# A gate matmul as seven products over halves of 256 tokens, with its weight parts made in gaps of GpSimd

## The reference, cut to what matters

```python
# x: (4096 tokens, 1024), float32; one layer
n = rmsnorm(h)
z = n @ w_in                                  # q, k, v, gates, and 4 x 512 columns of the convolution
y_gla  = rmsnorm(chunked_linear_attention(q, k, v, log_a)) * silu(g_gla)
y_conv = cb * causal_conv3(cc * cu) * silu(g_conv)
h = h + concat([y_gla, y_conv]) @ w_out
gate = sigmoid(h @ w_ple_gate + b_ple_gate)   # 1024 x 1024: what the change is about
h = h + gate * (p @ w_ple)                    # p has 256 columns
out = rmsnorm(h) * final_norm_w
```

## Time and profile before

| | us |
|---|---|
| median of three runs | 2034.15 (2034.09 to 2035.0) |
| the profiled execution, its own time | 2032.89 |
| its span | 2031.1 |
| TensorE busy | 1997.4 (98%) |
| VectorE / ScalarE / GpSimd busy | 1231.7 / 726.2 / 577.5 |

### The profile page before, as it was taken

One profiled execution on the slowest core, in us unless ns is written; L12 is line 12 of the kernel. 1 busy time (PEld: TensorE's weight loads), 2 busy tenths in 40 slices (PEclk: granted clock), 3 DMA queues, 4 the chain that ended last, 5 costly groups with the idle time before them and its releaser, 6 DMA issues.

```text
span 2031.1 us, 25878 instructions
## 1 busy us (share of the span) xinstructions
PE 1997.4 (98%) x9732; PEld 1665.8 (82%) x9732; DVE 1231.7 (61%) x1512; ACT 726.2 (36%) x1123; POOL 577.5 (28%) x590
## 2 busy tenths in 40 slices
PE   6999999999999999999999999999999999999997
PEld 5888888888888888888888888888888888888886
DVE  5766667666653576576576576567565355555553
ACT  5354354444433432332332332322322233333332
POOL 3766666666651112112112112144511000000000
PEclk9999999999999999999999999999999999999999
DMA  6345354454446312127312127486677322222111
GB/s 228 136 162 202 140 187 175 148 198 160 165 186 260 145 62 88 58 104 284 109 63 88 57 104 285 172 302 243 236 254 287 107 94 94 93 93 89 62 73 45
DMA packets 83991, 306.73 MB, mean 151 GB/s; under 512 B 10128, under 2 KB 20800, under 8 KB 73408
## 3 DMA queue, kind: packets, MB, share of 16 engines
q1 hardware_dynamic: 54752, 179.17, 24.2%
q0 software_dynamic: 29152, 126.40, 17.2%
HBM read 183.90 MB, written 121.63 MB: 150 GB/s over the span
## 4 chain that ended last, share of the span: by engine, by line
PE 96%; DVE 2%; ACT 1%; issue 1%; SPq 0%; DMA 0%; DVEq 0%; ACTq 0%
PE bank L1079 15%; PE bank L1085 15%; PE bank L1081 15%; PE bank L825 14%; PE bank L833 14%; PE bank L826 14%; PE bank L1166 1%; PE bank L1164 1%; PE bank L1165 1%; PE bank L912 1%; PE bank L972 1%; PE bank L963 1%; PE bank L856 1%; DVE XL L1581 1%; PE bank L857 1%
## 5 line engine op out<-in xcount | busy, mean ns | idle before, releaser
L1079 PE MATMUL bank<-XH,WC 128*128 128x512 f32 x1344 | 524.3, 390 | 0.1
L1085 PE MATMUL bank<-XL,WC 128*128 128x512 f32 x1344 | 523.0, 389 | 0.2 <-DVE XL L1747 0.2
L1081 PE MATMUL bank<-XH,WC 128*128 128x512 f32 x1344 | 522.9, 389 | 0.0
L1747 DVE TENSOR_TENSOR XL<-RQ,XH 128x1024 fp32r<-128x1024 f32 x168 | 220.0, 1344 | 230.4 <-ACT XH L1423 229.3
L1085 PEld LDWEIGHTS bank<-XL,WC 128*128 128x128 f32 x1344 | 252.3, 188 | 53.0 <-DVE XL L1747 0.6
L1079 PEld LDWEIGHTS bank<-XH,WC 128*128 128x128 f32 x1344 | 252.4, 188 | 52.3 <-issue 0.5
L1081 PEld LDWEIGHTS bank<-XH,WC 128*128 128x128 f32 x1344 | 252.4, 188 | 51.4
L763 POOL TENSOR_TENSOR RQ<-RQ 128x1024 f32<-128x1024 f32 x48 | 116.7, 2454 | 416.4 <-DVE RQ L1766 405.2
L1423 ACT ACTIVATE XH<-RQ 128x1024 fp32r<-128x1024 f32 x168 | 170.7, 1053 | 166.9 <-PE bank L1085 148.7
L825 PE MATMUL bank<-XH,WG 128*128 128x512 f32 x512 | 199.2, 389 | 0.0
L826 PE MATMUL bank<-XH,WG 128*128 128x512 f32 x512 | 199.2, 389 | 0.0
(11 more groups left out here) (185 smaller groups left out, 3330.0 us busy)
## 6 DMA issues: line engine op xcount, KB each, us to landing
WC<-w_scratch SPq DMA_DIRECT2D x21, 2048.0 KB, 8.8
RQ<-n_scratch POOLq DMA_DIRECT2D x32, 1024.0 KB, 5.5
w_scratch<-prep_hi POOLq DMA_DIRECT2D x84, 256.0 KB, 2.3
w_scratch<-PB POOLq DMA_DIRECT2D x84, 256.0 KB, 2.3
n_scratch<-raw SPq DMA_DIRECT2D x8, 2048.0 KB, 7.1
y_scratch<-y_sb SPq DMA_DIRECT2D x64, 256.0 KB, 2.8
RQ<-y_scratch POOLq DMA_DIRECT2D x16, 1024.0 KB, 6.3
xt<-xb_dram SPq DMA_DIRECT2D x64, 256.0 KB, 5.1
```

The costliest lines, as they stand in the source:

```text
L1079: nc.tensor.matmul(bank[:], WC[:, i, q, 0, k], xh, start=(k == 0 and i in (P1, P2, P5)), stop=False, skip_group_check=True)
L1081: nc.tensor.matmul(bank[:], WC[:, i, q, 1, k], xh, start=False, stop=False, skip_group_check=True)
L1085: mm = nc.tensor.matmul(bank[:], WC[:, i, q, 0, k], xl, start=False, stop=(k == 3), skip_group_check=True)
L1747: nc.vector.tensor_tensor(XL[:, k], RQ[:, OPERAND[s % 7], 2 * h:2 * h + 2], XH[:, k].bitcast(F32), ALU.subtract).then_inc(sx_lo, 1)
```

## The change

- The gate is computed per block of 512 tokens by the same seven products, over two halves of 256 tokens (`HT`) and two halves of the features. A matmul has 256 columns. `XHg` and `XLg` hold two operands each, over the old `XH` and `XL`. The tables T1 to T4 are made by VectorE in `TA` and `TB_`.
- The per-layer product is made in 8 units of 12 matmuls of 256 columns, two behind each of P2, P5, P3 and P4. A unit is two output tiles of one half of the tokens.
- Sums, sigmoids, mixing and squares go by unit. The loops over pairs of blocks are gone: all 8 blocks are written out.
- The gate's weights are now a fourth set of seven parts in `w_scratch`. The parts of P1, P2 and P4 are plain quarters; GpSimd makes them as 24 strips of 128x256, three in each convolution step (`strip`), in buffers over those of the heads' output. Those of P7, P6, P3 and P5 are made in steps 8 to 10 (`late_load`, `late_part`, 20 entries in the slots). The two tiles of `w_ple` follow in step 11 (`prep_tile`).
- In step 11 SyncE loads seven chunks of 2 MB and two of 1 MB.
- The statistics of the last block are one matmul after the last addition; before, seven of the eight squares went in earlier.

Core of the diff:

```diff
+HT = TB // 2
+GATE_A = (3, 4)
+GATE_C = (0, 1)
+PLE_BANK = (6, 7, 2)
+RESULT = ((0, 0), (1, 1), (1, 0), (0, 1))
...
-TILES = {GLA: 14, GATE: 16}
+TILES = {GLA: 14}
 PREP_STORES = (1, 1, 2, 2, 1, 7)
-GATE_TILES = PLE_K + KT
-GATE_SLOTS = {NB: (0, 0, 1), NB + 1: (1, 2, 1), NB + 2: (2, 2, 1)}
+PLAIN = ((P1, 0, 0), (P2, 0, 1), (P4, 1, 1))
+STRIPS = 4 * 2 * len(PLAIN)
+GATE_SLOTS = {NB: (1, 1, 1), NB + 1: (5, 3, 1), NB + 2: (5, 2, 1)}
+LATE_STORES = (0, 0, 2, 1, 1, 4)
 C_W0, C_W1, C_W2, C_GATED = range(1, 5)
...
@@ -459,14 +529,11 @@
                 if g % NP < NP - 1:
                     return
                 sp.wait_ge(sx_free, 4 * (7 * g + i + 1))
-                if g < STEPS - 1:
-                    if i == P1:
-                        wait_prepared(sp, g // NP + 2)
-                    load_weights(g // NP + 1, i)
-                elif i < 5:
-                    tile = WP[:] if i == 0 else WG[:, 2 * i - 2:2 * i]
-                    sp.dma_start(tile.bitcast(F32), g_scratch[i].rearrange("p (m h k c) -> p m h k c", m=2, h=2, k=KT)
-                                 ).then_inc(w_chunk[i], 16)
+                if i == P1:
+                    wait_prepared(sp, g // NP + 2)
+                    if g == STEPS - 1:
+                        sp.wait_ge(tile_stored, 16 * 2 * STRIPS)
+                load_weights(g // NP + 1, i)
...
-                    for half in range(2):
-                        sp.wait_ge(tile_lo_stored[half], 16 * GATE_TILES // 2)
+                    sp.wait_ge(tile_stored, 16 * 2 * (STRIPS + PLE_K))
...
+                if g == STEPS - 1:
+                    next_weights(g, P4)
+                    for part, tile in enumerate((WPH, WPL)):
+                        sp.dma_start(tile[:].bitcast(F32), g_scratch[part].rearrange("p (k m c) -> p k m c", k=PLE_K, m=KT)
+                                     ).then_inc(wp_loaded, 16)
...
                 for n in range(sum(counts), sum(counts) + GATE_SLOTS[g][slot_of]):
-                    prep_tile(n)
+                    if n % 5 == 0:
+                        late_load(n // 5)
+                    else:
+                        late_part(n // 5, n % 5 - 1)
...
+            def piece(n, src, raw_buf, hi_buf, hi_dst, lo_dst):
+                if n > 0:
+                    pool.wait_ge(tile_stored, 16 * 2 * n)
+                pool.dma_start(raw_buf, src).then_inc(tile_loaded, 16)
+                pool.wait_ge(tile_loaded, 16 * (n + 1))
+                pool.tensor_scalar(hi_buf, raw_buf, 1.0, 0.0, ALU.mult, ALU.add).then_inc(tile_split, 1)
+                pool.wait_ge(tile_split, 2 * n + 1)
+                pool.dma_start(hi_dst, hi_buf.bitcast(F32)).then_inc(tile_stored, 16)
+                pool.tensor_tensor(raw_buf, raw_buf, hi_buf.bitcast(F32), ALU.subtract).then_inc(tile_split, 1)
+                pool.wait_ge(tile_split, 2 * n + 2)
+                pool.dma_start(lo_dst, raw_buf).then_inc(tile_stored, 16)
+            def strip(n):
+                q, (i, tile, half), c = n // 6, PLAIN[n // 2 % 3], n % 2
+                if n == 0:
+                    for h in range(2):
+                        pool.wait_ge(y_stored[h], y_count(0))
+                at_col = half * TB + c * HT
+                to = 2 * q * TB + c * HT
+                piece(n, pair_tiles(3, q)[tile][:, at_col:at_col + HT], strip_raw[:], strip_hi[:],
+                      w_scratch[3, i, :, to:to + HT], w_scratch[3, i, :, to + TB:to + TB + HT])
+            def prep_tile(m):
+                if m == 0:
+                    wait_prepared(pool, 4)
...
                 difference(g, Q12, Q12, t3_made)
-                if g in GATE_SLOTS:
-                    prep_tiles(g, 0)
+                if is_conv(g):
+                    for n in range(3 * g, 3 * g + 3):
+                        strip(n)
+                elif g in GATE_SLOTS:
+                    gate_parts(g, 0)
+                elif g == STEPS - 1:
+                    for n in range(PLE_K):
+                        prep_tile(n)
                 split_waits(s + P6)
-                if g in GATE_SLOTS:
-                    prep_tiles(g, 1)
                 pool.wait_ge(t4_made, 2 * (g + 1))
                 difference(g, Q11, Q11, t1_made)
                 if g == STEPS - 1:
@@ -795,10 +934,12 @@
                 split_waits(s + P5)
                 load_quadrant(g + 1, Q11)
                 if g in GATE_SLOTS:
-                    prep_tiles(g, 2)
+                    gate_parts(g, 1)
                 split_waits(s + P3)
                 pool.wait_ge(t1_made, 2 * (g + 1))
                 load_quadrant(g + 1, Q22)
+                if g in GATE_SLOTS:
+                    gate_parts(g, 2)
                 split_waits(s + P4)
                 load_quadrant(g + 1, Q21)
...
+            def gate_product(b, i):
+                z = 7 * b + i
+                banks = GATE_A if i in (P1, P6, P7, P4) else GATE_C
+                for q in range(4):
+                    if b == 0 and q == 0:
+                        pe.wait_ge(w_chunk[i], 16 * 4)
+                    if q % 2 == 0:
+                        wait_gate_bank(b, i, q // 2)
+                    if q == 0:
+                        pe.wait_ge(gx_hi, z + 1)
+                    acc_ap = ps[banks[q // 2]][:, q % 2 * HT:q % 2 * HT + HT]
+                    for k in range(4):
+                        xh, xl = XHg[:, z % 2, k], XLg[:, z % 2, k]
+                        nc.tensor.matmul(acc_ap, WC[:, i, q, 0, k], xh, start=(k == 0 and q % 2 == 0 and i in (P1, P2, P5)),
+                                         stop=False, skip_group_check=True)
+                        nc.tensor.matmul(acc_ap, WC[:, i, q, 1, k], xh, start=False, stop=False,
+                                         skip_group_check=True)
+                        if q == 0 and k == 0:
+                            pe.wait_ge(gx_lo, z + 1)
+                        mm = nc.tensor.matmul(acc_ap, WC[:, i, q, 0, k], xl, start=False, stop=(k == 3),
+                                              skip_group_check=True)
+                    mm.then_inc(g_prod, 1)
...
+            def gate(b):
+                gate_product(b, P1)
+                gate_product(b, P6)
+                if b > 0:
+                    out_stats(b - 1)
+                gate_product(b, P7)
+                for c, i in enumerate((P2, P5, P3, P4)):
+                    gate_product(b, i)
+                    ple_unit(b, 2 * c)
+                    ple_unit(b, 2 * c + 1)
...
+            def gate(b):
+                z = 7 * b
+                gate_hi(z + P6)
+                gate_copy(b, P1, 0)
+                gate_copy(b, P1, 1)
+                gate_hi(z + P7)
+                gate_copy(b, P6, 0)
+                gate_copy(b, P6, 1)
+                gate_hi(z + P2)
+                split_p_hi(b)
+                if b > 0:
+                    nc.scalar.preload_act_table_set(LOG_EXP)
+                    out_rms(b - 1)
+                gate_hi(z + P5)
+                sigmoid(b, 0)
+                gate_copy(b, P7, 0)
+                sigmoid(b, 1)
+                gate_copy(b, P7, 1)
+                gate_hi(z + P3)
+                gate_square(b, 0)
+                gate_square(b, 1)
+                sigmoid(b, 2)
+                sigmoid(b, 3)
+                gate_hi(z + P4)
+                gate_square(b, 2)
+                gate_square(b, 3)
+                sigmoid(b, 4)
+                sigmoid(b, 5)
+                gate_hi(z + 7)
+                sigmoid(b, 6)
+                gate_square(b, 4)
+                sigmoid(b, 7)
+                if b == NB - 1:
+                    nc.scalar.preload_act_table_set(LOG_EXP)
+                gate_square(b, 5)
+                gate_square(b, 6)
+                gate_square(b, 7)
             def out_rms(b):
...
+            def gate(b):
+                z = 7 * b
+                gate_lo(z + P6)
+                gate_lo(z + P7)
+                gate_t1_t4(b)
+                gate_lo(z + P2)
+                split_p_lo(b)
+                if b > 0:
+                    dve.wait_ge(out_rstd, b)
+                    final_norm(b - 1, range(4))
+                gate_lo(z + P5)
+                if b > 0:
+                    final_norm(b - 1, range(4, 8))
+                gate_sum(b, 0)
+                gate_sum(b, 1)
+                gate_lo(z + P3)
+                gate_mix(b, 0)
+                gate_mix(b, 1)
+                gate_sum(b, 2)
+                gate_sum(b, 3)
+                add_square(b, 1)
+                gate_lo(z + P4)
+                gate_mix(b, 2)
+                gate_mix(b, 3)
+                gate_t3(b + 1)
+                gate_sum(b, 4)
+                gate_sum(b, 5)
+                add_square(b, 3)
+                gate_lo(z + 7)
+                gate_mix(b, 4)
+                gate_mix(b, 5)
+                gate_t2(b + 1)
+                add_square(b, 4)
+                add_square(b, 5)
+                gate_mix(b, 6)
+                gate_mix(b, 7)
```

(81 more changed lines are left out.)

556 lines of the change are left out of this document (322 added, 234 removed).

## The result

| | before | after |
|---|---|---|
| median of six runs each, us | 2034.12 (2032.46 to 2036.19) | 2049.28 (2044.16 to 2050.46) |
| ratio to before | | 1.0071 (95% interval 1.0058 to 1.0084) |
| span of the profiled execution | 2031.1 | 2048.4 |

What follows compares the result with a forecast made beforehand. The prediction took TensorE's own stream, 96% of the chain, as the bound. Its terms -20.5 + 17.8 + 2.0 + 4.8 + 3.6 gave +7.7 us, 2042 us against 2034.15, 0.4% slower, range 2034 to 2059.

Steps and rivals of the forecast that it cites:

- its own case: Whole kernel: the forecast's terms as summed, 2042 us, with 2036 to 2049 for this case alone; chance kept 0.55.
- a gate whose pace VectorE sets: Gate: a wait in front of one VectorE sum holds all behind it, +17 us, 2059; chance 0.10.
- the rival at 2049: Convolution: strips' instructions beside VectorE's additions delay P1, 1 us in each of seven steps, 2049; chance 0.08.
- The gate's stream, -20.5: Gate: 432 matmuls at 0.120 us replace 240 at 0.2267, a gain of 2.56 us per block, 20.5 over eight.
- The rivals at 0.127 and at 0.109: Gate: 256-column matmuls take 0.127 us (2065, chance 0.05), or 0.109 with next to no fixed part (2004, chance 0.02).
- Step 0, +17.8: Convolution step 0: stores of heads and three strips delay T1 in GpSimd's queue; P5 starts 17.8 us later, bounds 16.5 and 25.5.
- The clock, +2.0: After TensorE's idle time in step 0: about four us at half speed lose 2.0 us, bounds 0 and 5.
- Later steps, 0: Convolution steps after step 0 and up to the gate: strips and late parts fit GpSimd's gaps, loss 0, bounds 0 and 3.
- Block ends, +4.8: Gate, seven block boundaries: VectorE's chain to P6's low part ends late, stalling TensorE 0.7 us each, 4.8 in all.
- The tail, +3.6: After the last product: table load and VectorE's chain delay the final statistics, 3.6 us lost, bounds 2.5 and 5.
- "No difference": Whole kernel: block ends and clock cost nothing, the rest holds, 2035; chance 0.15.
- the short wait in step 0: Convolution step 0, GpSimd's queue: a strip takes 3.3 us, not 6.9; stall 7, clock full, 2029; chance 0.05.

Runs made afterwards that it cites:

- experiments 1 to 3: 1: kernel after, no strip in step 0, four in steps 1 to 6, 2029.07 us; 2: kernel before plus only the stores' wait, 2035.89; 3: kernel after, one strip, 2034.48.
- Experiment 5: Kernel after without step-0 strips (four in steps 1 to 6), and GpSimd's first late part of the third group moved from step 9's end to step 10's gap: 2024.23 us.

## Why the forecast held, and where it was off

- **The range**: the measured median is in it, but above what the forecast gave its own case. The range reached up to 2059 for a gate whose pace VectorE sets, and that did not happen; that it also covered a wait in step 9 was luck. So was the match with the rival at 2049, which puts its loss into the seven steps behind step 0.
- **What bounds the kernel**: right. The difference is in starts of matmuls that came late or lay closer, and in the tail behind the last, and the busy share of TensorE (98% before, 97% after) tells none of it.
- **The gate's stream, -20.5**: right to 0.1 us. The gate's 422.36 is 432 x 0.120 x 8 = 414.7, the statistics 3.2 and 4.6 for the boundaries. The rivals at 0.127 and at 0.109 are both out; 0.120 holds over thousands of pairs. The rule of the Trainium skill (TensorE: Matmul & The Clock Gate, section Back-to-back issue gap), N / 2.4 + 2.5 ns, given there for an isolated matmul, does not hold for these in their stream at the higher clock: it gives 109.2 and 215.8 ns where 120 and 227 are measured. Its N / 1.2 for the lower clock, 426.7 ns for 512 columns, the trace does bear out: starts at 0.43 us behind the wait of step 0.
- **Step 0, +17.8**: mechanism right, shown by experiments 1 to 3; size 20.2, within the bounds of 16.5 and 25.5 (by the forecast's own terms the lower one comes to 16.8). Of the 2.4 missing, 1.0 are the strips: 7.25, 7.4 and 5.5 where 6.9, 6.9 and 5.2 were taken, with issue, landing and the idle time behind a rounding each a tenth or two longer. The first began 41.6 us behind the start of the step where 40.8 was forecast: the last head's store landed about 0.3 later, and the load was issued 0.5 behind the landing. And TensorE was through with P2 0.4 us earlier than before, so its wait is longer by that.
- **The clock, +2.0**: 1.5, what P5 of step 0 loses. But the forecast had the clock fall only there, and it fell behind the shorter wait of 3.4 us at 1454 too (next term). The lower bound of 0 is out.
- **Later steps, 0**: the term that failed. The forecast asked only whether the late parts end before GpSimd's own next duty ("the other slots fit within a us") and not whom they hold up while they run. The part in front of T3 held VectorE's low parts and additions, those T2 and the last sums, and those P1 of step 10: 5.05 us, 3.4 of waiting and 1.65 by the lower clock behind it. The rival of strips that hold VectorE named that mechanism, but put it beside the strips, whose instructions are short. There it costs little: steps 1 to 8 lose 0.4 us in this kernel, all in P1 of step 1, and 0 to 0.7 us in the variants. Experiment 5 shows that the part at that place is the cause; that VectorE stands still beside GpSimd is read from the durations. The rule of the Trainium skill (SBUF — State Buffer, section SBUF: two separate sides), by which one of the two holds a shared pair of ports for a whole instruction and an addition of VectorE takes part only if both of its inputs lie in SBUF, agrees with both readings: 10.78 for `xt<-xt,EB`, 2.47 for `xt<-xt,bank`. Whether VectorE gets its turn between two instructions of GpSimd the rule leaves open; the addition of 6.89 us did not get one between three that followed each other.
- **Block ends, +4.8**: 4.6. The chain was the one described.
- **The tail, +3.6**: 4.3. The table load was in the chain (1.4), and the last matmuls ran at half the clock, 2.08 us for two where 1.12 stood before.
- **The other rivals**: VectorE doesn't set the pace of the gate; no product but P6 waits in it. "No difference" and the short wait in step 0 are excluded by the interval and by the 20.1 us.
- **Sum**: -20.5 + 20.2 + 1.5 + 5.05 + 4.6 + 4.3 = +15.1. Of the 7.4 missing in the forecast 5 are the late parts and 2.4 the wait of step 0; the other errors (-0.5, -0.2, +0.7) cancel.

## What to carry to other kernels

Work put into an engine's idle gap costs in two ways: by what stands behind it in that engine's queue, and by whom it slows while it runs; ask both for each gap, the first of a series above all, where the pipeline is not yet in its rhythm. The arithmetic gain of this change (4.7% of the gate's stream) was real and was outweighed by four waits, each of which a few lines of order took away. When the spread of runs is several us, an account by stretches of one bottleneck engine's starts tells single microseconds.
